# Input rows in a buffer per block, adaLN strips between the first sums and units, and the samples' depthwise convolution on TensorE

## The reference, cut to what matters

```python
def modulate(x, g, shift, scale):          # shift, scale: chunks of silu(c) @ w_ada + b_ada
    return rmsnorm(x, g) * (1 + scale[:, None, :]) + shift[:, None, :]

def conv_module(h, prev, w_pw1, b_pw1, w_dw, b_dw, ln_g, ln_b, w_pw2):
    a = h @ w_pw1 + b_pw1
    u = a[..., :D_MODEL] * jax.nn.sigmoid(a[..., D_MODEL:])
    up = jnp.concatenate([prev.astype(u.dtype), u], axis=1)     # prev: 30 cached rows of each sample
    y = lax.conv_general_dilated(up, w_dw[:, None, :].astype(up.dtype), (1,), 'VALID',
                                 dimension_numbers=('NWC', 'WIO', 'NWC'),
                                 feature_group_count=D_MODEL) + b_dw     # depthwise, 31 taps
    y = jax.nn.silu(layernorm(y, ln_g, ln_b))
    return y @ w_pw2, up[:, -(CONV_W - 1):]
```

## Time and profile before

| | us |
|---|---|
| median of 3 runs | 1907.1 (1903.12 to 1909.9) |
| the profiled execution | 1907.56 |
| its span in the trace | 1905.9 |
| first product of the first unit (L1444) | 73.12 |
| mean of the LayerNorm ready (L759) | 357.78, and 0.66 long |

### The profile page before, as it was taken

The page is one execution under the profiler, slowest core; times in us unless marked ns, Lnnn a source line. Parts: engine busy times, 40 slices in busy tenths (PEclk is TensorE's granted clock), DMA queues, the critical chain, the costliest instruction groups (busy, mean ns, idle before and its releaser), DMA issues.

```text
span 1905.9 us, 30256 instructions
## 1 busy us (share of the span) xinstructions
PE 1679.4 (88%) x12409; PEld 1488.9 (78%) x12409; DVE 914.8 (48%) x1618; ACT 561.5 (29%) x1058; POOL 270.9 (14%) x384
## 2 busy tenths in 40 slices
PE   5788874497999999997988989988897999999995
PEld 2666653397999999997887965454497999999994
DVE  1479999755323232335224246756645323223333
ACT  2332221333222122222221355544423222122222
POOL 1002939120000000000210034432300000000000
PEclk8899987698999999998899999978998999999997
DMA  9399983051233222321322240020221233222311
GB/s 311 157 348 341 307 278 102 0 137 56 78 97 92 66 79 85 107 64 34 100 73 56 77 121 23 1 68 23 67 68 55 78 95 94 63 82 82 110 32 50
DMA packets 236591, 198.10 MB, mean 104 GB/s; under 512 B 6999, under 2 KB 196127, under 8 KB 236253
## 3 DMA queue, kind: packets, MB, share of 16 engines
q1 hardware_dynamic: 230448, 172.54, 29.4%
q0 software_dynamic: 5840, 23.30, 3.9%
q10 hardware_dynamic: 173, 0.39, 0.1%
HBM read 188.88 MB, written 11.20 MB: 105 GB/s over the span
## 4 chain that ended last, share of the span: by engine, by line
PE 71%; DVE 11%; issue 8%; ACT 4%; DMA 3%; DVEq 1%; POOL 1%; SPq 1%; ACTq 0%; POOLq 0%
PE ps L1444 58%; PE ps L1426 4%; PE ps L1752 2%; PE ps L1705 2%; DMA ada<-in_w_ada_dram 2%; DVE y L1117 2%; DVE wl L971 1%; PE ps L1631 1%; DVE r L1117 1%; PE ps L1472 1%; DVE r L995 1%; PE ps L1822 1%; DVE y L1122 1%; PE ps L1607 1%; DVE t L1005 1%
## 5 line engine op out<-in xcount | busy, mean ns | idle before, releaser
L1444 PE MATMUL ps<-Hh,wh 128*128 128x288 f32 x2128 | 470.8, 304 | 67.9 <-DVE Hl L1010 40.8
L1444 PE MATMUL ps<-Hl,wh 128*128 128x288 f32 x2128 | 465.4, 301 | 0.0
L1444 PE MATMUL ps<-Hh,wl 128*128 128x288 f32 x2128 | 464.2, 300 | 0.0
L646 ACT ACTIVATE wh<-raw 128x1024 fp32r<-128x1024 f32 (+1 forms) x173 | 192.9, 1116 | 828.2 <-PE ps L1444 805.8
L1444 PEld LDWEIGHTS ps<-Hh,wh 128*128 128x128 f32 x2128 | 351.5, 194 | 71.9 <-issue 70.5
L1444 PEld LDWEIGHTS ps<-Hl,wh 128*128 128x128 f32 x2128 | 351.9, 193 | 0.2
L1444 PEld LDWEIGHTS ps<-Hh,wl 128*128 128x128 f32 x2128 | 351.5, 193 | 0.2
L971 DVE TENSOR_TENSOR wl<-raw,wh 128x1024 fp32r<-128x1024 f32 (+1 forms) x173 | 225.1, 1301 | 255.5 <-ACT wh L646 255.0
L1444 PE MATMUL ps<-ah,wl 128*128 128x288 f32 x704 | 150.8, 296 | 0.0
L1444 PE MATMUL ps<-ah,wh 128*128 128x288 f32 x704 | 150.8, 296 | 0.0
L1444 PE MATMUL ps<-al,wh 128*128 128x288 f32 x704 | 150.7, 296 | 0.0
(11 more groups left out here) (273 smaller groups left out, 1958.5 us busy)
## 6 DMA issues: line engine op xcount, KB each, us to landing
ada<-in_w_ada_dram SPq DMA_DIRECT2D x64, 1024.0 KB, 7.6
raw<-in_ffn_w_up_dram SPq DMA_DIRECT2D x88, 512.0 KB, 3.8
raw<-in_ffn_w_down_dram SPq DMA_DIRECT2D x32, 704.0 KB, 4.6
raw<-in_conv_w_pw_dram SPq DMA_DIRECT2D x24, 512.0 KB, 8.5
raw<-in_w_kv_dram SPq DMA_DIRECT2D x12, 512.0 KB, 3.7
C<-in_cache_kv_dram POOLq DMA_DIRECT2D x32, 128.0 KB, 4.1
raw<-in_nsa_w_in_dram SPq DMA_DIRECT2D x8, 512.0 KB, 3.8
Cs<-in_cache_kv_dram SPq DMA_DIRECT2D x16, 256.0 KB, 3.9
```

The source lines that it names most:

```text
L646: A(wh[:, u % RING, 0:K, 0:w], raw[:, u % RING, 0:K, 0:w], ACT.Copy).then_inc(hi_ready, 1)
L1444: last = M(ps[0:w, 2 * s + h, 0:HT], wt[:, s, k, 0:w], rt[:, k, h * HT:(h + 1) * HT], start=(k == 0 and i == 0), stop=(k == K - 1 and i == 2))
```

## The change

- Each block of x has a buffer of its own: two in `stage`, three in `xrows`, which lies where `Hl` comes later. POOL issues the five loads at once; the two of the conv cache wait for the turning of blocks 0 and 1. PE turns all five blocks before the first strip.
- SP issues the conditioning rows and three pieces of w_ada ahead of the small vectors, a fourth ahead of the weights, and 15 pieces before its loop over the units.
- PE's order in the head is: blocks 0 to 4, strip 0, the vectors, strip 1, three sums, strip 2, five sums, blocks 5 and 6, strip 3, strip 4. The sums of the first norm lie in banks 4 and 5. Strip 5 lies in the middle of the first triple. The reciprocal of the first norm comes before the wait for the strips.
- The samples' convolution leaves POOL and DVE for PE. `us4` holds, for chunk j and each group g of 32 channels, four copies of its rows of `u_s` shifted by 0, 1, 2 and 3 tokens, one in each 32-partition group; 16 transfers, issued by POOL, make them. `taps4` holds the taps on the diagonal of 32-column matrices, made by one POOL instruction for each j from `sel32` and `wd4`. `sample_conv(j)` is 8 steps by 4 groups of products (128 rows, 32 columns, 64 tokens), which ACT moves out with the bias. Chunk j is done after unit 2j + 5; chunks 6 and 7 after the last strip.
- The sums of the LayerNorm wait for all eight chunks of the samples. `norm(k)` no longer waits for POOL's convolution. The two transfers from DRAM to DRAM are issued after the last strip.

```diff
+CONV_AT = {2 * j + 5: j for j in range(DC - 2)}
-SMP_CONV = [(0, 4), (4, 7)]
+STEPS = (CW + 3) // 4
-STRIP_BLOCKS = [1, 2, 3, 4]
-STRIP_PLAN = [1, 1, 0] + [2] * 13
+ROW_BUF = [0, 1, 2, 3, 4, 0, 1]
+ROW_BANK = [0, 1, 2, 0, 1, 0, 1]
+STRIP_PLAN = [0, 0, 1] + [2] * 12 + [1]
+        xrows = at("xrows", [P, 3, D], rH + DC * T * 4)
+        us4 = at("us4", [P, 4, (CW - 1 + NT) * NB], rF + ...)
+        taps4 = at("taps4", [P, 2, 4, STEPS, 32], rG)
...
 # SP
+            while n_ada < RING_ADA:
+                load_ada(sp, n_ada)
+                n_ada += 1
...
-            while n_ada < 2 * STRIPS_FIRST + RING_ADA:
+            load_ada(sp, n_ada)
+            n_ada += 1
+            for u in range(RING):
+                load_unit(sp, u)
+            while n_ada < 2 * (STRIPS_FIRST + 2) + RING_ADA:
...
 # POOL
+            nc.gpsimd.memset(wd4[:], 0.0).then_inc(S("wd4"), 1)
...
+            for j in range(DC):
+                if j >= 2:
+                    pool.wait_ge(S("cs_pe"), j - 1)
+                nc.gpsimd.tensor_tensor(taps4[:, j % 2], sel32[:].unsqueeze(1).unsqueeze(1).to_broadcast([P, 4, STEPS, 32]),
+                                        wd4[:, :, :, j:j + 1].to_broadcast([P, 4, STEPS, 32]), ALU.mult).then_inc(S("taps_in"), 1)
+                pool.wait_ge(tile_free, 2 * (j + 1))
+                if j:
+                    pool.wait_ge(S("cs_pe"), j)
+                for g in range(4):
+                    for sh in range(4):
+                        n = (CW - 1 + NT - sh) * NB
+                        pool.dma_start(us4[32 * sh:32 * sh + 32, g, 0:n],
+                                       u_s[32 * g:32 * g + 32, j, sh:, :].rearrange("p t b -> p (t b)")).then_inc(S("us4_in"), 16)
+            pool.wait_ge(ada_used, 2 * N_STRIP)
...
-                nc.gpsimd.tensor_tensor(ysmp[:, cs], u_s[:, cs, 0:NT, :], bc(wdT[:, c0:c1]), ALU.mult).then_inc(step, 1)
-                for k in range(1, CW):
...
 # ACT
+            def sample_out(j):
+                act.wait_ge(S("cs_pe"), j + 1)
+                A(y[:, j, TP:T].rearrange("p (b t) -> p t b", b=NB), ps[:, 7, TS:2 * TS].rearrange("p (t b) -> p t b", b=NB),
+                  ACT.Identity, bias=vT[:, R_BDW + j:R_BDW + j + 1]).then_inc(S("cs_ev"), 1)
...
 # DVE
-                    V.scalar_tensor_tensor(acc_s, u_s[:, j, 2:2 + NT, :], wj[2], acc_s, ALU.mult, ALU.add).then_inc(taps_s, 1)
...
 # PE
+            def sample_conv(j):
+                pe.wait_ge(S("taps_in"), j + 1)
+                pe.wait_ge(S("us4_in"), 16 * 16 * (j + 1))
+                for i in range(STEPS):
+                    for g in range(4):
+                        last = M(ps[32 * g:32 * g + 32, 7, TS:2 * TS], taps4[:, j % 2, g, i, :],
+                                 us4[:, g, 4 * i * NB:(4 * i + NT) * NB], start=(i == 0), stop=(i == STEPS - 1))
+                last.then_inc(S("cs_pe"), 1)
...
+            dense(0, Hh, Hl, normed(0), tiles=RING, midway=next_strip)
             for u in range(U_PW2):
...
+                if u in CONV_AT:
+                    pe.wait_ge(ada_ev, 4 * (s_ - 1))
+                    sample_conv(CONV_AT[u])
+                    convs += 1
...
+            for j in range(DC - 2, DC):
+                if j == DC - 1:
+                    pe.wait_ge(S("cs_ev"), DC - 1)
+                sample_conv(j)
...
+            pe.wait_ge(S("cs_ev"), DC)
```

More of the change, by code:

```diff
@@ L96 @@
 STRIPS_FIRST = 4
[L97 to L100 removed]
+ROW_BUF = [0, 1, 2, 3, 4, 0, 1]
+ROW_BANK = [0, 1, 2, 0, 1, 0, 1]
+STRIP_PLAN = [0, 0, 1] + [2] * 12 + [1]
+assert len(STRIP_PLAN) == U_PW2 and sum(STRIP_PLAN) + 2 == N_STRIP - STRIPS_FIRST
 RING_ADA = 3
@@ L315, in build @@
         sel = place("sel", [P, 1 + NB])
+        sel32 = place("sel32", [P, 32])
+        wd4 = place("wd4", [P, 4, STEPS, DC])
         peb = place("peb", [P, 2])
@@ L383, in build, with rows_in @@
         xi_rows = [P, P, P, P, TS, 120, 120]
+        def rows_in(bk):
+            n, k = xi_rows[bk], ROW_BUF[bk]
+            return stage[0:n, k, :] if k < 2 else xrows[0:n, k - 2, :]
         page_rows = a["cache_kv"].rearrange("n (q e) t h d -> n q e (t h d)", e=2)
@@ L505, in load_rows @@
                     src = a["state_conv"].rearrange("l b t d -> (l b t) d")[120 * (bk - 5):120 * (bk - 4), :]
-                pool.dma_start(stage[0:n, bk % 2, :], src).then_inc(S(f"xi_in{bk % 2}"), 16)
-            load_rows(0)
-            load_rows(1)
+                pool.dma_start(rows_in(bk), src).then_inc(S(f"xi_in{ROW_BUF[bk]}"), 16)
+            for bk in range(5):
+                load_rows(bk)
             nc.gpsimd.memset(ones[:], 1.0).then_inc(S("const"), 1)
@@ L666, in root @@
                 act.wait_ge(S("st_ck"), sums_done(st))
-                A(halves(r[:]), stats, ACT.Sqrt, scale=1.0 / D, bias=epst[:]).then_inc(S("st_rms"), 1)
+                A(halves(r[:]), stats if st else stats0, ACT.Sqrt, scale=1.0 / D, bias=epst[:]).then_inc(S("st_rms"), 1)
             def square(st, m):
@@ L692, in _ @@
             A(rows0[0:72, 4, :], rows0[0:72, 4, :], ACT.Silu).then_inc(S("c_silu"), 1)
-            for u in range(SPLIT_AHEAD):
-                split_hi(u)
-            act.wait_ge(S("vec_pe"), 2)
+            act.wait_ge(S("c_pe"), 1)
             act.wait_ge(S("const"), 4)
@@ L708, in block_out, with square0 @@
                 A(dst, src, ACT.Copy).then_inc(S("xi_act"), 1)
+            def square0(c0, c1):
+                for cc in range(c0, c1):
+                    A(sqb[:, cc, :], x[:, cc, :], ACT.Square).then_inc(S("st_sq"), 1)
             for bk in range(5):
                 block_out(bk)
[L712 to L717 removed]
+            strip_out(0, None)
             act.wait_ge(S("xi_dve"), 5)
             act.wait_ge(S("xi_act"), 5)
[L720 to L721 removed]
+            act.wait_ge(S("vec_dve"), 3)
+            square0(0, 3)
+            strip_out(1, 0)
+            square0(3, 8)
+            for u in range(SPLIT_AHEAD):
+                split_hi(u)
+            strip_out(2, 1)
             block_out(5)
@@ L1488, in _, with block_in, sums0 @@
             pe.wait_ge(S("id_in"), 32)
+            pe.wait_ge(S("c_silu"), 1)
+            tr(ps[:, 6, 0:72], rows0[0:72, 4, :]).then_inc(S("c_pe"), 1)
+            def block_in(bk):
+                n = xi_rows[bk]
+                pe.wait_ge(S(f"xi_in{ROW_BUF[bk]}"), 16 * (1 + bk // 5))
+                if ROW_BANK[bk] in ROW_BANK[:bk]:
+                    before = max(k for k in range(bk) if ROW_BANK[k] == ROW_BANK[bk])
+                    pe.wait_ge(S("xi_dve"), before + 1)
+                    pe.wait_ge(S("xi_act"), before + 1)
+                for cc in range(DC):
+                    last = tr(ps[:, 2 * ROW_BANK[bk] + cc // 4, (cc % 4) * n:(cc % 4 + 1) * n],
+                              rows_in(bk)[:, cc * P:(cc + 1) * P])
+                last.then_inc(S("xi_pe"), 1)
+            def sums0(c0, c1):
+                for cc in range(c0, c1):
+                    pe.wait_ge(S("st_sq"), cc + 1)
+                    sum_chunk(sqb[:, cc, :], cc, S("st_ck"), bank=4)
+            for bk in range(5):
+                block_in(bk)
+            pe.wait_ge(S("const"), 4)
+            pe.wait_ge(S("vec_act"), 1)
+            strip(0)
             pe.wait_ge(S("vec_in"), 16 * 11)
```

183 lines of the change are left out of this document (73 added, 110 removed).

## The result

| | before | after |
|---|---|---|
| median (range, runs) | 1906.6 (1903.1 to 1909.9, 4) | 1886.3 (1879.2 to 1891.2, 4) |
| the profiled execution, its span | 1907.6, 1905.9 | 1887.9, 1886.2 |
| first product of the first unit | 73.12 | 67.16 |
| mean of the LayerNorm ready | 358.43 | 338.46 |

What follows compares the result with a forecast made beforehand. DVE, lengthened by POOL from 24.0 to 35 us a chunk, was taken to bound the convolution, transfers the head. Mean at 306 against 358.4, and 1.4 from second sums, gave -54 us: 1854, range 1846 to 1864 (8 in 10: 1838 to 1880).

Steps and rivals of the forecast that it cites:

- Where the work lies: Whole kernel: the change works in the first 358 us; the 1549 us behind the LayerNorm's mean stay as they are.
- The head: Start of the kernel, bound by transfers: first unit at 53 us against 73.1, bounds 48 and 58.
- rival (d): Head: it gains nothing, since the ring's refill gaps eat the gain; 1874 us, chance 0.04.
- Triple and unit 3: First triple and GLU: unit 3 starts at about 83 us, where before it was 104.5.
- Units 3 to 14: Twelve units with two strips each: 14.2 us a unit, between 13.4 and 16.0, 170 us in all.
- rival (a): Units: PE carries new work on top of transfer waits; 16.0 us each, 1876 us (0.20), or 1904 with dear `sample_conv` (0.03).
- The sign that I gave for it: Units 3 to 14: a DMA share well under 1 and PE full would show PE's work adding to its waits.
- Rival (b): Units and tail: copies cost the transfers nothing and their tail is short; 13.4 us a unit, 1840 us, chance 0.14.
- POOL's part: Units: POOL's taps product of 2.7 to 5.4 us and sixteen issues at 0.53 to 0.64 us stay hidden.
- rival (c): POOL's copy issues wait behind DVE's instructions: 1884 us with one wait each (0.04), beyond 1908 (0.03).
- The tail: End of the stage: POOL's last copies are late, the mean's sums start at 295, mean ready at 306 against 358.4.

Runs made afterwards that it cites:

- e1: The kernel after with the first three pieces of w_ada issued behind the small vectors instead of ahead of them; 1885.2 us.
- e6: The kernel after with all eight sums of x and blocks 5 and 6 ahead of strip 2, and ACT's root ahead of its copies for strips 2 and 3; 1882.8 us.
- e9: e5 without the 128 copies into `us4`, so the samples' convolution multiplies zeros; 1845.2 us.
- e8: The kernel after with e2, e5 and e6 together, and cached-row turnings and seven of eight mean sums ahead of the last chunk's products; 1876.1 us.
- e3: The kernel after without the 128 copies into `us4`, so the samples' convolution multiplies zeros; products stay; 1864.8 us.
- e4: The kernel after with one of the eight steps of each `sample_conv`, the copies staying; 1882.5 us.
- e5: The kernel after with `sample_conv` ahead of its unit's last strip instead of behind that strip and its turning; 1881.0 us.
- e12: e8 with the shifted copies into `us4` written by ACT in place of the transfers, everything computed; 1848.9 us.
- e2: The kernel after with the taps product moved from POOL to DVE, behind the chunk's last addition; 1876.7 us.
- e11: e5 with the shifted copies into `us4` written by ACT in place of the transfers, everything computed; 1854.6 us.

## Why the prediction was wrong, step by step

**Where the work lies.** Right: the stages behind the mean did not move, and the mean waits for ACT's last sample chunk and that for POOL's copies, not for DVE.

**The head (+14.2).** The step that failed is "The last piece lands at 49. Behind it come its products (1.1), ACT's copy (0.6), the samples' Hh (0.63) and the first chunk's (0.72) and DVE's low part (0.75): first unit at 53". Of the 14.2 us, 5.8 are the strip's start in this execution: I put the cost of the ring at 3 us of refill gap and did not ask what PE does between strips 2 and 3 (6.8 us of sums and 1.8 of blocks, while the three pieces of the ring came in and lay ready). The other 8.4 are the chain behind it. I left out that bank 7 holds one strip, so that turning 2, ACT's four biases, turning 3 and again biases follow one another (56.6 to 61.6, with the copies of blocks 5 and 6, a table load and the root, 4.0 us together, ahead of them in ACT's queue), and then DVE's three instructions of 0.69 us for the samples. e1 shows that the vectors' place alone is no cause; e6 gives no gain from the sums' place that stands out of the scatter. The chain is the part that all executions share: e9, with the head of after, starts strip 3 at 49.6, as forecast, and its first unit still comes 12.4 us later.
```profile
49.58 1.92 PE L1483 MATMUL ps<-ada,cpad 128*32 128x512 f32 x16
...
61.96 0.82 PE L1470 MATMUL ps<-Hh,wh 128*128 128x288 f32 x2 [2.72 <-DVE Hl L1045]
```
With e8's order the second piece is multiplied at 50.6, and the first unit starts at 63.8: the chain is the larger part. How much of the 5.8 us belongs to the order, and how much to this execution, stays open. So rival (d), a head that gains nothing, was half right: 6 of its 20 us came.

**Triple and unit 3 (+0.3).** Right to 0.3 us, from rows of before.

**Units 3 to 14 (+16.2).** The step that failed is the choice between PE's 13.8 and the transfers' 14.1 us a unit as if the slower of the two set the pace; 15.5 is their interplay. Of the 31.1 us of a chunk, 28.0 are there with neither the late convolution nor the copies (e9). The late place adds 3.0 (e3 against e9): 1.38 of waiting, which I had put at 1.0, and about 1.6 for a half unit that takes 4.9 (e3) or 5.0 (after) in place of 3.3 us at the lower clock, which I had at nothing. That the clock falls was in the rows of before for a wait at the end of the stage (4.93 us for 12 products), and I used it there but not here. The size of `sample_conv`, 1.7 us by a row of the same shape, was right (1.1 to 1.9), and e4 shows that it hardly matters: without seven eighths of it the half unit behind was slower by 0.6 us.
The copies I had at 0.9 us a unit, by their bytes. With the late convolution they cost nothing more in the profiled executions (31.0 and 31.1), though 21 us by the medians, of which the end explains 10. With the early one they cost 5.3 us a chunk in place of 1.8, by e5 against e9. So in the traces either edit alone shows no gain in the pace, and both together show 3 us a chunk. What I also left out is DVE. I gave it slack because its chunk takes 24 us against 28.4; in e9 and e12 it never idles, and 28.0 on PE is not what ends the stage there.
This is rival (a), PE's new work on top of its waits, which I had at 0.20 with 16.0 us a unit; measured 15.5. I gave it 1876, because I kept the head at 53; with the head's 14.2 us and the units' 16.2 it comes to 1884. The sign that I gave for it was not met: the DMA share stayed at 0.97, and PE was busy 27.9 of 31.1 us. Rival (b), copies that cost nothing and 13.4 us a unit, is out: even without any copy a unit is 14.0.

**POOL's part.** The issues are right, 0.49 us each beside DVE, so rival (c) is out. The product is wrong. Its range came from 0.51 us for 192 elements "alone" and 1.01 beside DVE, but at 319.26 DVE was at work too, so neither row is a time alone:
```profile
319.23 1.08 DVE L1109 SCALAR_TENSOR_TENSOR y<-u_p,wdT,y 128x512 f32<-128x512 f32 x1
```
The product alone takes 1.96 us. 2.7 to 5.4 us were forecast, and it took 9.2 to 16 beside DVE's taps, which stay at 0.75 us in an unbroken row; only DVE's addition at the end of the row is stretched (2.33 us, in e2 0.69). In e5 it goes the other way in five of the seven chunks (in the other two the product took 14.5 and 15.6). There POOL's product takes 1.98 us beside such a row, and a DVE instruction is stretched, here a tap to 3.60:
```profile
210.31 3.60 DVE L1154 SCALAR_TENSOR_TENSOR r<-u_p,wdT,r 128x512 f32<-128x512 f32 x1
```
```profile
211.37 1.98 POOL L553 TENSOR_TENSOR taps<-sel,wd 128x1024 f32<-128x1024 f32 x1
```
So one of the two waits for the other, and which one differs, from kernel to kernel and within e5. By the Trainium skill, "SBUF — State Buffer", section "Who interferes with whom", a DVE instruction with two SBUF inputs and a GpSimd one that reads SBUF contend, and the order of issue decides who blocks. I took from it that DVE stops for 2.7 us; e5 agrees (2.9), and the trace of after shows the other outcome, in which POOL lost up to 14 us. The same section has ACT wait for nobody, and e11 and e12 agree: 0.445 us a copy beside a DVE that is busy 30.97 of 31 us.

**The tail (+1.9).** The net is close by luck. The last copies were to be issued as soon as `us4` was free; behind POOL's product they came 8.2 us later (e2 takes 6 us off the mean). I also left out the turnings of the cached rows behind the last wait (3.3 us). Against that, 16 issues took 7.9 us, not 9.6, the last landing 1.3 us behind them, not 3, both of these twice, and the sums of the mean took 7.93 us, not 9.9, since PE was at work before them.

**What stays open.** Why the median of e3 lies 14 us under its profiled execution, and what makes the first unit start 6 us apart in kernels with the same head. Why the copies, 0.6 MB a chunk, hold the pieces up by more than their share: the share of POOL's queue of the 16 engines rose from 3.9% before to 4.9% in after, which is 2.4 us a chunk, and the rest of the 5.3 I put down to waits and clock from windows like those of e5, but no run separates them.

## What to carry to other kernels

Where two limits stand close together, don't just take the larger: ask what the waits of one add to the other, and price a wait of PE twice, once as idle time, once as the products behind it at the lower clock. Test such a pair by removing both, since removing either alone shows less than its share; then look which engine is full, for the next limit (DVE here) may be close. Small copies between partitions were cheaper here on an engine with time to spare (ACT) than on the queues that feed the bound; and an operand that POOL makes beside a long DVE row may come only when that row ends. Marks of one execution scatter by some us: compare them with a kernel whose code in that place is the same before calling a difference an effect.

## What the runs showed of the hardware that I had not expected

- A POOL product of 1024 elements with two SBUF inputs: 1.96 us alone (after, at 55 us); beside back-to-back DVE instructions of two inputs either 9.2 to 16 us with the taps undisturbed (seven of seven in after), or 1.98 us with one DVE instruction at 3.60 in place of 0.74 (e5). On DVE it takes 1.22 us (e2).
- 128 transfers of 35 to 38 KB, each over 32 partitions, cost 36 us by the medians of e5 and e9 (21 by those of after and e3), the longer end of the stage included, against 0.6 MB a chunk that would be 1.8 us by bytes.
- The granted clock fell to 0.63 over 5 us after 1.4 us of waiting with 64 narrow products behind it, to 0.55 over 5.6 us with 8 of them (e4), and to 0.53 for 10 us after a wait of 4.5 (e5); in e9, with the same narrow products ahead of a strip and no wait before them, it was 1.00 over both windows shown.
- On SP's queue, behind 3 MB of loads just issued, one issue took 4.5 us and two later ones 5.1 together; in e1, ahead of those loads, 0.4 and 0.8.
- ACT moves 32 partitions by 280 to 304 elements to another partition group in 0.445 us on average (e12), beside a DVE that is busy 30.97 of 31 us.
